# Block 2's gate projections as split float32r products, with the state projection and its scans moved ahead

## The reference

```python
x = x + 0.5 * swiglu_ffn(rms_norm(x, ffn1_norm), ffn1_w_in, ffn1_w_out)
h = rms_norm(x, mix_norm)
q_a, k_a, v_a, q_i, k_i, w_i, u_s, q_m, gates = split(h @ w_in)      # 1476 + 3 * 1024 columns
q_a, k_a = rms_norm(q_a by heads), rms_norm(k_a)
o_a = indexed_sparse_attention(q_a, k_a, v_a, q_i, k_i, w_i, rel_bias) @ w_o_a   # 64 keys chosen by index scores
y_s = gelu(s5_layer(u_s, ...))                                         # complex linear recurrence over time
glu_a, glu_b = split(y_s @ w_glu);  o_b = glu_a * sigmoid(glu_b)
o_m = memory_attention(rms_norm(q_m), m_k, m_v) @ w_o_m
g = sigmoid(gates by 3 branches)
merged = g[0] * o_a + g[1] * o_b + g[2] * o_m
x = x + merged @ w_out
x = x + 0.5 * swiglu_ffn(rms_norm(x, ffn2_norm), ...);  x = rms_norm(x, final_norm)
```

## Time and profile before

| | |
|---|---|
| median of 3 runs | 2253.45 us (2252.74 to 2255.07) |
| the profiled execution | 2257.1 us, its span 2255.3 us |
| TensorE busy | 2177.9 us, 97% |
| VectorE busy | 1556.7 us, 69% |
| ScalarE busy | 1179.6 us, 52% |
| Pool busy | 170.4 us, 8% |
| granted TensorE clock, mean | 0.986 |
| block 2's projections | about 1825 to 1968 us of the span |
| attention heads to x updated | about 1968 to 2057 us |

### The profile page before, as it was taken

One profiled execution on the slowest core, in us unless ns is written; L12 is line 12 of the kernel. 1 busy time (PEld: TensorE's weight loads), 2 busy tenths in 40 slices (PEclk: granted clock), 3 DMA queues, 4 the chain that ended last, 5 costly groups with the idle time before them and its releaser, 6 DMA issues.

```text
span 2255.3 us, 32139 instructions
## 1 busy us (share of the span) xinstructions
PE 2177.9 (97%) x12243; PEld 1836.1 (81%) x12243; DVE 1556.7 (69%) x1678; ACT 1179.6 (52%) x1194; POOL 170.4 (8%) x242
## 2 busy tenths in 40 slices
PE   8989999998899999999999999999899999989998
PEld 7878888897778888888888888888688878877886
DVE  3655453465488888989898988889765426867453
ACT  4133443313267777777777777777564322355442
POOL 1200000320300000000000000000075010200000
PEclk9999999999899999999999999999999999999999
DMA  9123555422379999999999999999656554425552
GB/s 346 61 94 121 187 186 185 140 71 94 108 282 366 358 361 350 358 349 361 349 362 348 361 371 348 368 347 363 253 168 191 173 149 150 150 86 167 186 186 75
DMA packets 251028, 537.26 MB, mean 238 GB/s; under 512 B 18006, under 2 KB 140928, under 8 KB 250560
## 3 DMA queue, kind: packets, MB, share of 16 engines
q1 hardware_dynamic: 246800, 521.11, 65.2%
q0 software_dynamic: 3168, 9.07, 1.6%
q10 hardware_dynamic: 976, 5.91, 0.6%
HBM read 534.71 MB, written 1.31 MB: 238 GB/s over the span
## 4 chain that ended last, share of the span: by engine, by line
PE 85%; DVE 8%; issue 3%; ACT 2%; DMA 1%; DVEq 0%; SPq 0%; ACTq 0%
PE bank L1245 9%; PE bank L1247 9%; PE bank L1246 9%; PE bank L1372 7%; PE bank L1373 7%; PE bank L1376 7%; PE bank L997 6%; PE bank L1498 5%; PE bank L1387 4%; PE bank L1388 4%; PE bank L1392 4%; PE bank L1188 2%; DVE weights_lo L2228 2%; PE bank L1347 1%; DVE arena L2431 1%
## 5 line engine op out<-in xcount | busy, mean ns | idle before, releaser
L2228 DVE TENSOR_TENSOR weights_lo<-ring_data,weights_hi 128x2048 fp32r<-128x2048 f32 x336 | 759.2, 2289 | 89.9 <-ACT weights_hi L1940 88.0
L1940 ACT ACTIVATE weights_hi<-ring_data 128x2048 fp32r<-128x2048 f32 x336 | 636.9, 1918 | 162.8 <-DMA ring_data<-in_moe_w 161.6
L1372 PE MATMUL bank<-weights_hi,xg_hi 128*128 128x512 f32 x896 | 351.9, 393 | 4.0 <-DVE arena L2638 2.6
L1373 PE MATMUL bank<-weights_hi,xg_lo 128*128 128x512 f32 x896 | 349.0, 389 | 0.0
L2223 DVE TENSOR_TENSOR weights_lo<-ring_data,weights_hi 128x2048 fp32r<-128x2048 f32 x98 | 228.8, 2365 | 51.6 <-ACT weights_hi L1727 51.6
L1376 PE MATMUL bank<-weights_lo,xg_hi 128*128 128x512 f32 x896 | 239.7, 389 | 0.0
L1246 PE MATMUL bank<-weights_lo,xT_hi 128*128 128x512 f32 x584 | 228.7, 392 | 0.0
L1245 PE MATMUL bank<-weights_hi,xT_hi 128*128 128x512 f32 x520 | 206.3, 397 | 1.0 <-DVE xT_lo L2216 0.6
L1247 PE MATMUL bank<-weights_hi,xT_lo 128*128 128x512 f32 x520 | 203.1, 391 | 0.0
L1372 PEld LDWEIGHTS bank<-weights_hi,xg_hi 128*128 128x128 f32 x896 | 168.3, 188 | 38.7 <-issue 3.0
L1376 PEld LDWEIGHTS bank<-weights_lo,xg_hi 128*128 128x128 f32 x896 | 168.2, 188 | 35.2
(11 more groups left out here) (462 smaller groups left out, 3201.7 us busy)
## 6 DMA issues: line engine op xcount, KB each, us to landing
ring_data<-in_moe_w SPq DMA_DIRECT2D x672, 512.0 KB, 4.3
ring_data<-in_ffn_w_in SPq DMA_DIRECT2D x88, 512.0 KB, 4.7
ring_data<-in_w_in SPq DMA_DIRECT2D x70, 512.0 KB, 4.5
ring_data<-in_ffn_w SPq DMA_DIRECT2D x66, 512.0 KB, 4.0
ring_data<-in_ffn_w_out SPq DMA_DIRECT2D x44, 512.0 KB, 3.9
ring_data<-in_w_out SPq DMA_DIRECT2D x24, 512.0 KB, 4.3
ring_data<-in_w_in SPq DMA_DIRECT2D x8, 396.0 KB, 4.1
ring_data<-in_w_in SPq DMA_DIRECT2D x8, 390.0 KB, 5.3
```

The costliest lines, as they stand in the source:

```text
L1372: mm(o, xg_hi[:, k, :], e_hi(at)[:, r], start=k == 0, stop=False)
L1373: mm(o, xg_lo[:, k, :], e_hi(at)[:, r], start=False, stop=False)
L1940: nc.scalar.activation(e_hi(at), ring_data[:, e_slot(at), :], ACT.Copy).then_inc(ring.hi_done, 1)
L2228: v.tensor_tensor(e_lo(at), ring_data[:, e_slot(at), :], e_hi(at), ALU.subtract).then_inc(ring.lo_done, 1)
```

## The change

The twelve gate slots leave `PROJ2`. They become twelve ring slots of their own, each half of the rows (512) by 512 columns, two to a chunk of 512 columns. Each is split: `gate_high(t)` on ScalarE, `gate_low(t)` on Pool for all twelve (`POOL_GATE_LOWS = 12`; the loop for VectorE is empty), and the activations too (`gx_hi` on ScalarE, `gx_lo` on Pool in two halves, over `actT`, once all other projections are done). TensorE multiplies in three products into four banks, each 512 columns wide. High parts have two buffers in turn, so `gate_high(t)` waits until slot t - 2 is used.

The state projection comes first in `PROJ2`, its products before the index keys, and VectorE does the rotations and scans first of all, in groups of four (1024 elements) with scratch `turn_tmp` that overlaps `gates`; index selection comes second, the heads' norm third. The heads' transposes stand after gate slot 10 of 12. On Pool the bias additions come ahead of the memsets. `tail_high(2)` and `tail_low(2)` move behind the heads.

```diff
-PROJ2 = [(C_QI, 256, "qi"), (C_KI, 68, "kiw"), (C_QA, 256, "qa"), (C_QA + 256, 256, "qa"), (C_KV, 128, "kv"),
-         (C_US, 256, "us"), (C_QM, 256, "qm")] + [(C_G + 256 * i, 256, "gate") for i in range(12)]
+PROJ2 = [(C_US, 256, "us"), (C_QI, 256, "qi"), (C_KI, 68, "kiw"), (C_QA, 256, "qa"), (C_QA + 256, 256, "qa"), (C_KV, 128, "kv"),
+         (C_QM, 256, "qm")]
+GATE_CHUNKS = 6
+GATE_SLOTS = 2 * GATE_CHUNKS
+POOL_GATE_LOWS = 12
...
+            for t in range(GATE_SLOTS):
+                c, half = C_G + 512 * (t // 2), t % 2
+                ring2.load(sp, N_GATE + t, slots_of(N_GATE + t, 4), a["w_in_2"][0][512 * half:512 * half + 512, c:c + 512].rearrange("(k p) c -> p k c", p=P))
...
+            def gate_low(t):
+
+                pool.wait_ge(sem("gate_hi"), t + 1)
+                nc.gpsimd.tensor_tensor(gate_lo(t), ring2.slot(N_GATE + t), gate_hi[t], ALU.subtract).then_inc(sem("gate_lo"), 1)
+
+            for t in range(2):
+                gate_low(t)
+            pool.wait_ge(sem("gx_hi"), 1)
+            pool.wait_ge(ring2.used, N_GATE)
+            for half in range(2):
+                k = slice(4 * half, 4 * half + 4)
+                nc.gpsimd.tensor_tensor(gx_lo[:, k, :], actT[:, k, :], gx_hi[:, k, :], ALU.subtract).then_inc(sem("gx_lo"), 1)
+            for t in range(2, POOL_GATE_LOWS):
+                gate_low(t)
+            pool.wait_ge(sem("bias_loaded"), 256)
+            pool.wait_ge(sem("dve_stage"), stage("keys_chosen"))
+            for h in range(AH):
+                nc.gpsimd.tensor_tensor(bias[:, h, :], bias[:, h, :], score, ALU.add).then_inc(sem("bias_ready"), 1)
+
+            pool.wait_ge(sem("bias_ready"), AH)
             pool.wait_ge(sem("qT_psum"), 3)
             st.do(nc.gpsimd.memset(qaz[0][HD:P, :, :], 0.0))
...
+                def gate_slot(t):
+
+                    c, half = t // 2, t % 2
+                    pe.wait_ge(sem("gate_hi"), t + 1)
+                    if half == 0 and c < 2:
+                        proj2_out(pe, len(PROJ2) - 2 + c)
+                    elif half == 0:
+                        pe.wait_ge(sem("gate_out"), c - 1)
+                    w_hi, w_lo = (w.rearrange("p (k c) -> p k c", k=4) for w in (gate_hi[t], gate_lo(t)))
+
+                    def products(x, w, start=False, stop=False):
+                        for j in range(TT):
+                            for k in range(4):
+                                i = mm(bank[2 * (c % 2) + j][:, :], x[:, 4 * half + k, P * j:P * j + P], w[:, k, :], start=start and k == 0, stop=stop and k == 3)
+                        return i
+
+                    products(gx_hi, w_hi, start=half == 0)
+                    if t < 2:
+                        pe.wait_ge(sem("gate_lo"), t + 1)
+                        products(gx_hi, w_lo)
+                        pe.wait_ge(sem("gx_lo"), t + 1)
+                        i = products(gx_lo, w_hi, stop=half == 1)
+                    else:
+                        products(gx_lo, w_hi)
+                        pe.wait_ge(sem("gate_lo"), t + 1)
+                        i = products(gx_hi, w_lo, stop=half == 1)
+                    i.then_inc(ring2.used, 1)
...
+                for t in range(GATE_SLOTS - 2):
+                    gate_slot(t)
+                pe.wait_ge(sem("idx_rel"), IH)
                 pe.wait_ge(sem("dve_stage"), stage("heads_normed"))
...
+                for t in range(GATE_SLOTS - 2, GATE_SLOTS):
+                    gate_slot(t)
...
+                def gate_high(t):
+
+                    ring2.arrived(act, N_GATE + t)
+                    if t >= 2:
+                        act.wait_ge(ring2.used, N_GATE + t - 1)
+                    if t >= 8 and t % 2:
+                        act.wait_ge(sem("dve_stage"), stage("states_ready"))
+                    nc.scalar.activation(gate_hi[t], ring2.slot(N_GATE + t), ACT.Copy).then_inc(sem("gate_hi"), 1)
+
+                def gate_chunk(c):
+
+                    act.wait_ge(ring2.used, N_GATE + 2 * c + 2)
+                    if c == 0:
+                        act.wait_ge(sem("dve_stage"), stage("states_ready"))
+                    for j in range(TT):
+                        a_(gates[:, c, j, :], bank[2 * (c % 2) + j][:, :], ACT.Sigmoid, "gate_out" if j == TT - 1 else "act_steps", scale=rowm[:, j:j + 1])
...
+                project(6)
+                for c in range(GATE_CHUNKS - 1):
+                    if c == 3:
+                        act.wait_ge(sem("dve_stage"), stage("heads_sumsq"))
+                        a_(rq[:, :], ssq[:, :], ACT.Sqrt, "act_stage", scale=1.0 / HD, bias=NORM_EPS)
+                    gate_high(2 * c + 2)
+                    gate_high(2 * c + 3)
+                    gate_chunk(c)
...
+                dve.wait_ge(sem("pool_stage"), stage("powers_ready"))
+                t0, t1, t2 = (turn_tmp[:, i] for i in range(3))
+                for sign in (-1, 1):
+                    for g in range(2):
+                        if sign < 0:
+                            dve.wait_ge(sem("bu_act"), 4 * g + 4)
+                        js = slice(4 * g, 4 * g + 4)
+                        c, s, br, bi = Ct[:, js, :], St[:, js, :], bu[:, js, 0, :], bu[:, js, 1, :]
+                        st.do(tt(t0, br, s, ALU.mult))
...
```

More of the change, by code:

```diff
@@ L602, in two_block_kernel, with gate_lo @@
         DENSE_SPLIT = (0, 1, 3)
-        MIX_SEQ = [i for i, (_, _, kind) in enumerate(PROJ2) if kind in ("qi", "kiw", "us")]
+        DVE_SEQ = [i for i, (_, _, kind) in enumerate(PROJ2) if kind in ("us", "qi", "kiw")]
+        ACT_SEQ = [i for i, (_, _, kind) in enumerate(PROJ2) if kind not in ("us", "qi")]
         def proj2_out(eng, m):
-            eng.wait_ge(sem("proj2_act"), len([i for i in range(m + 1) if i not in (MIX_SEQ[0], MIX_SEQ[2])]))
-            if m >= MIX_SEQ[0]:
-                eng.wait_ge(sem("proj2_dve"), len([i for i in MIX_SEQ if i <= m]))
+            eng.wait_ge(sem("proj2_dve"), len([i for i in DVE_SEQ if i <= m]))
+            if m >= ACT_SEQ[0]:
+                eng.wait_ge(sem("proj2_act"), len([i for i in ACT_SEQ if i <= m]))
+        def gate_lo(t):
+            return lo_slots[:, (N_GATE + t + ring2.shift) % RING, :]
         def plain(u):
@@ L913, in _ @@
             pool.wait_ge(sem("pool_stage"), stage("queries_zeroed"))
[L914 to L917, removed]
             pool.wait_ge(sem("merged_ready"), 2)
@@ L1501, in branches @@
                 project(0)
                 spread_rows()
+                turn_blocks()
                 project(1)
[L1504 to L1513, removed]
@@ L2059, in branches @@
                 a_(row_bc, bank[7][:, 0:T], ACT.Copy, "act_stage")
-                for m in range(1, 3):
-                    project(m)
+                act.wait_ge(sem("rms_sq"), 2 * TT)
+                act.wait_ge(sem("xT_dve"), 2 * plain(T_MIX))
+                a_(gx_hi[:, :, :], actT[:, :, :], ACT.Copy, "gx_hi")
+                for j in range(NS):
+                    act.wait_ge(sem("bu_psum"), j + 1)
+                    a_(bu[:, j], bk(4 + j % 4, 2, T), ACT.Copy, "bu_act")
+                project(2)
+                project(3)
                 act.wait_ge(sem("pe_stage"), stage("mkT_psum"))
                 a_(mkT[:, :, :], bk(4, 2, T), ACT.Copy, "act_stage")
-                for m in (3, 4, 6):
-                    project(m)
+                gate_high(0)
+                project(4)
+                gate_high(1)
+                project(5)
                 for h in range(IH):
@@ L2068, in branches @@
                     a_(rel[:, h, :], bk(4 + h, 3 * P), ACT.Relu, "idx_rel", scale=HD ** -0.5 * IH ** -0.5)
-                for j in range(NS):
-                    act.wait_ge(sem("bu_psum"), j + 1)
-                    a_(bu[:, j], bk(4 + j % 4, 2, T), ACT.Copy, "bu_act")
-                act.wait_ge(sem("dve_stage"), stage("heads_sumsq"))
-                a_(rq[:, :], ssq[:, :], ACT.Sqrt, "act_stage", scale=1.0 / HD, bias=NORM_EPS)
-                for m in range(7, 13):
-                    project(m)
+                project(6)
+                for c in range(GATE_CHUNKS - 1):
[5 more added lines that the diff above has]
+                    gate_chunk(c)
+                act.wait_ge(sem("dve_stage"), stage("states_ready"))
+                tail_high(0)
                 act.wait_ge(sem("qT_psum"), 3)
@@ L2082, in branches @@
                 a_(kaT, bank[7][:, 0:T], ACT.Copy, "qT_act")
-                def tail_high(t):
-                    ring2.arrived(act, N_OA + t)
-                    nc.scalar.activation(tail_hi[t], ring2.slot(N_OA + t), ACT.Copy).then_inc(ring2.hi_done, 1)
-                for m in range(13, len(PROJ2)):
-                    project(m)
-                    if m == len(PROJ2) - 3:
-                        tail_high(0)
-                    if m == len(PROJ2) - 2:
-                        act.wait_ge(sem("dve_stage"), stage("states_ready"))
-                        tail_high(1)
-                        tail_high(2)
```

(8 more changed lines are left out.)

165 lines of the change are left out of this document (89 added, 76 removed).

## The result

The changed kernel takes 2261.29 us (median of 7 runs, 2256.16 to 2265.55); the kernel before, run beside it, 2255.07 (7 runs, 2252.74 to 2258.36). Ratio 1.0027, 95% interval 1.0017 to 1.0037: slower by 6.2 us, where a shift of 6.4 was forecast. The interval lies clear of 1, though 0.27% is little.

A forecast was written before the change was run, and what follows sets the result against it. TensorE, busy 97%, was taken as the bound: -17.6 us of gate work, + (4.2 + 1.2 + 2.8 + 1.6 + 11.7) of waits, + 2.0 of clock; shift +6.1, plus 0.3 for Sigmoids: 2253.45 + 6.4 = 2259.9 us. Range for 8 in 10: 2244 to 2272.

The forecast's parts named there:

- TensorE's own work: Gate slots on TensorE: 24 float32r matmuls, 5.45 us a slot instead of 6.91, 17.6 us less for twelve.
- Gates start: First gate slot on TensorE: still starts at about 1883.4, 0.3 us later than before.
- Exclusion, one VectorE operation per Pool instruction: Gates, Pool beside VectorE: each holds for a whole instruction, so one VectorE operation per Pool subtraction of 4.6 us.
- States_ready: VectorE's state work: done at 1906.3 instead of 1883 uncontended, with 23.2 us of Pool's operations against it.
- Waits at slot 4: TensorE before and in gate slot 4: idle 4.2 us, then 1.2 more for Pool's low part.
- Waits at slot 8: TensorE before and in gate slot 8: idle 2.8 us, then 1.6 for Pool's low part.
- Heads_normed and the wait before the transposes: VectorE's heads' norm ends at 1959.3; TensorE idles 11.7 us before the heads' transposes, slots 10 and 11 behind.
- Clock: TensorE after the long wait: three to four us at half speed cost 2.0 us, bounds 0 and 4.
- Behind the scores: From the scores on nothing else moves, except ScalarE's last Sigmoids of 512, which add 0.3 us.
- Rival 1: Pool and VectorE in the gates hardly exclude each other: shift -12.9, 2240.5 us; chance 0.27 with its milder form.
- Rival 2: VectorE's index selection is excluded by Pool's subtractions too: heads_sumsq at 1944, 2271 us; chance 0.14.
- Rival 3: Exclusion holds, but heads_sumsq doesn't hold gate_high(8); only the heads wait remains: 2253 to 2256 us; chance 0.14.

The follow-up runs named there:

- writes_only: Changed kernel with each of Pool's twelve subtractions replaced by three memsets, for timing alone; span 2248.5 us in one run, ratio not given.
- pool_halves: Changed kernel with each of Pool's twelve subtractions of 2048 issued as two of 1024; ratio 1.0019 to the kernel before.
- transposes_last: Changed kernel with the heads' transposes after all twelve gate slots instead of after ten; ratio 1.0009 to the kernel before.
- lows8: Changed kernel with low parts 8 to 11 on VectorE behind the heads' norm, Pool keeping 0 to 7; 2253.9 us, ratio 0.9983 to the kernel before.
- kiw_later: Changed kernel with the index keys' slot moved from behind the state products to behind kv; ratio 1.0012 to the kernel before.
- lows8_kiw_later: Changed kernel with the edits of lows8 and kiw_later together; ratio 0.9983 to the kernel before.
- high_first: Changed kernel with ScalarE's high part of slot 4 ahead of the first Sigmoids, slot 8's ahead of the square root; ratio 1.0045 to the kernel before.
- lows8_spread: lows8 with ScalarE's order of high_first, and VectorE's low parts 8 and 9 spread ahead of and inside the norm; 2249.67 us, ratio 0.9974 to the kernel before.

## Why the prediction was right, step by step

- **TensorE's own work**: slots of 5.44 us (5.45 forecast); right.
- **Gates start**: +0.3 forecast, +4.1 in the profile. Left out were the two short waits in the state products (1.4 together, partly made up) and the clock behind them. Five kernels with the same order started their gates at +0.8 or +0.9, so what the clock takes on top of theirs is between nothing and 3.3 from one execution to the next. I had all of it at nothing.
- **Exclusion, one VectorE operation per Pool instruction**: the premise that decided the sign. writes_only and pool_halves show both halves of it, reads and turns. I had one thing too narrow: it isn't two inputs alone. A COPY of 64 elements and a TENSOR_SCALAR of 384 were blocked as well. The Trainium skill ("SBUF — State Buffer", Who interferes with whom) names copy and tensor_scalar in the 2-port modes among those that contend; the trace agrees, 4.62 and 3.50 us. This enters the sum little, since the forecast had counted the last compare and every short operation of the norm as blocked. One reading was off: a bias addition takes 0.99 to 1.02 us alone (writes_only), not the 0.9 scaled from 1024 elements.
- **States_ready**: 1906.3 forecast, 1908.7 measured, 1907.0 on the old clock. Right.
- **Waits at slot 4**: 4.2 + 1.2 forecast, 2.2 + 0.8 measured. The gates had started 3.8 later and took up that much of it; ScalarE's table load for the Sigmoids, 1.28 us behind the same wait, gave some back. It was not in the sum.
- **Waits at slot 8**: 2.8 + 1.6 forecast, 1.3 + 1.0 measured. The first is shorter by what TensorE was still late. The second doesn't depend on that: Pool's low part came 5.0 after the high part, not 5.2, and TensorE's first two thirds took 4.0, not 3.6. Heads_sumsq came at 1933.8 on the old clock, 1932.9 forecast, but by other blocks than the forecast's: the index scores ran free, and the compare (3.50 for 0.36) and a product of 128 elements (4.68 for 0.28) were blocked.
- **Heads_normed and the wait before the transposes**: 1959.3 and 11.7 forecast, 1961.4 (1959.7 on the old clock) and 11.4 measured. transposes_last, whose scores come 8.2 us earlier (not all by the edit), shows that it costs because two slots are queued behind it, and lows8 that it goes when Pool is idle during the norm.
- **Clock**: 2.0 forecast. Transposes and two slots, 12.4 us at full clock, took 15.0 from 1961.59 to 1976.62: 2.6. The windows show 0.82 there.
```profile
1950.00:1961.50 11.50, 0.18 (x1) 0.00 (x0) 11.46 (x7) 4.86 (x4) 11.11 (x7) 0.64 0.25 91
1961.50:1976.60 15.10, 15.01 (x62) 12.86 (x63) 4.43 (x2) 5.86 (x8) 8.82 (x8) 0.82 0.20 69
```
- **The sum**: forecast 0.3 - 17.6 + 21.5 + 2.0 = +6.2. Measured 4.1 - 17.7 + 16.7 + 2.6 = +5.7, and the scores at +7.3; the 1.6 left is in the restarts, which were not priced. Thirds follow each other at 1.81 us. Around each of the four waits in the slots some 0.3 is lost: slot 4 starts 2.36 later than it could have, of which the row counts 2.20 as idle, and its first third takes 1.94. The first third of all takes 0.2 more, and 0.2 is lost ahead of the transposes. Start too early by 3.8 and waits too long by 4.8 all but cancelled. The near-equality of the two sizes is luck, but that they offset each other is not: kiw_later, lows8_kiw_later and high_first show that TensorE's start and the short waits hardly move the end, since VectorE's chain to heads_normed sets it.
- **Behind the scores**: +0.3 forecast, -0.7 measured; the cause stays open.

The forecast was made for the median, and the terms are checked on the slowest execution. In a faster one the gates may start some 3 us earlier and the waits be longer; no profile of the changed kernel shows that.

**Rival 1** (hardly any exclusion) fell; writes_only shows that nearly without it the span is 6.8 shorter than before, not the 12.9 worked out: the wait for Pool is 7.8, not 4.5 (the eight bias additions took 10.64, not 7.2, one of them 3.05 beside a subtraction of VectorE's), and the stretch behind the scores is 1.8 longer. **Rival 2** (selection excluded too) fell. Pool was busy for 12.7 of the 15 us of this window, and the eight rounds, 11.50 us before, took 11.50:
```profile
1911.00:1926.00 15.00, 12.02 (x53) 9.61 (x53) 14.37 (x53) 7.49 (x7) 12.74 (x3) 1.00 0.45 140
```
```profile
1912.24 0.62 DVE L2925 MAX8 small<-arena 128x8 f32<-128x128 f32 x2
...
1922.31 0.62 DVE L2925 MAX8 small<-arena 128x8 f32<-128x128 f32 x2
1923.74 3.50 DVE L2930 TENSOR_SCALAR arena<-arena 128x384 f32<-128x384 f32 x1
```
The Trainium skill's sentence quoted there ("VectorE: DVE Perf Modes", Two Vector instructions with no wait between them) says one input each, and the trace agrees with what was made of it: MATCH_REPLACE didn't wait. Neither did MAX8, which the sentence doesn't name. **Rival 3** fell: heads_sumsq did hold gate_high(8), for 1.3 us.

## What to carry to other kernels

Work handed to an idle Pool isn't free when it reads SBUF: count the VectorE operations beside it, give each the length of one Pool instruction, and see which chain they belong to. Keep Pool's subtractions from the short chains (here the norm): eight of twelve on Pool were faster than before, twelve slower, each by 0.2 to 0.3%. Beside selection they cost VectorE nothing; putting more of them there was not tried. And follow the chain that ends last, not the idle times: three changes of order that took waits or low clock from TensorE (kiw_later, high_first, lows8_spread) moved its scores by 0 to 2 us.

## What the runs showed of the hardware

- A COPY of 64 float32 elements, 0.19 us alone, took 4.62 beside Pool's subtraction of 2048 and 2.37 beside one of 1024. Memsets of Pool left VectorE's 1.22 us operations with two inputs at 1.22, but one such COPY took 1.66, to the end of the memsets (writes_only).
- MAX8 and MATCH_REPLACE rounds of 1.44 us kept their pace beside Pool's subtractions.
- The granted clock was 0.71 over 16 us in which TensorE was never idle, behind narrow products and two waits under 0.8 us, and 0.92 over the same 16 us of lows8, with the same instructions: 3.3 us apart.
